# The pairwise adds of x squared, moved from VectorE to GpSimd in a fused two-layer kernel

## The chip, the cores and the metric
One core of one Trainium2 chip runs the kernel. The metric is device time in microseconds of one execution, the median of several runs. TensorE does the matrix products, VectorE and ScalarE the elementwise work, GpSimd (POOL in the rows) here only issues transfers, and SyncE (SP) issues most of the loads.

## What is computed
The input x has 512 tokens of 2048 features; it is kept as 16 tiles of 128 features by 512 tokens. Two layers follow each other. The first normalises x and mixes it with window means:

```python
h = rms_norm(x) * (1.0 + scale) + shift          # scale, shift, gate come from c @ w_mod
u, g = jnp.split(h @ w_in, 2, axis=-1)
pooled = windows' means of u minus u             # 4 groups, windows 2, 4, 8, 16
y = einsum(pooled, w_grp) * pool_scale
x = x + gate * ((y * silu(g)) @ w_out)
```

The second has three attentions, one of which reads 256 memory tokens:

```python
mkv = rms_norm_2(mem, mem_norm_gain) @ w_mem_kv
mk, mv = jnp.split(mkv, 2, axis=-1)              # 4 heads of 128; mk is normalised per head
```

What this case is about is the beginning: the eight panels of the product for mk and mv (the memory panels), and beside them the sum over the features of x * x, which `rms_norm(x)` of the first layer needs.

## The kernel before
Every weight is an fp32 panel that comes in four quarters of 128 by 512. A quarter is split into a rounded high part, made by ScalarE (`split_hi`, line 406), and a rest, made by VectorE (`split_lo`, line 416). TensorE then does three products for each 128 by 128 tile (`tile_products`, lines 422 to 424): high by high, high weight by low input, low weight by high input. The split runs three quarters ahead of its use: `split_hi` for quarter s waits until TensorE has used quarter s - 4, and `split_lo` waits for `split_hi`. Both engines work through their instructions strictly in the order in which the program lists them; semaphores join the engines.

At the start there are eight memory panels, n = 0 to 7; four give keys (one head each) and four give values. Each panel has four steps, s = 0 to 3, on each engine. I call the stretch of one panel on VectorE a beat. For n from 1 to 4 VectorE does in a beat:

- s = 0: `split_lo`; `mem_result` scales the product of the panel before (line 1659, `mem_plain`); from n = 2 `mem_keys` finishes the key norm (lines 473 and 475) and writes `mem_out` (line 1676).
- s = 1: `split_lo`, then `mod_column`, one product with a row sum over 2048 columns (lines 1614 and 1615), for the modulation of the first layer.
- s = 2: `split_lo`, then `mem_variance` (line 1608), whose drain is line 1669.
- s = 3: `split_lo`, then `add_square_of_x(2n - 1)` (line 1682).

ScalarE's beat has the four `split_hi`, the squares of a key panel (line 1251), two squares of x (`square_of_x(2n - 2)` and `(2n - 1)`, line 1265; each covers two tiles of x, 128 by 1024) and, at s = 3, `rstd_guess`, three instructions of lines 464, 466 and 468 that wait for the variance. In `x_squares` there are four places. The add number p = 1, 3, 5, 7 adds square p onto square p - 1.

TensorE sums each added pair over the features with a matrix of ones: `x_pair(j)` of line 1060 runs in panel n = j + 2 between its first and second quarter, and waits for `x_square_added` to reach j + 1. After the fourth, VectorE makes the variance of x in panel 5, ScalarE its root (`rstd_guess`), and in panel 6 VectorE scales the first tiles of x by it. TensorE cannot start the first layer's products (the `front` stage) without these.

GpSimd's queue at this time: the constants, the row of c, then a loop over the eight stores of keys and values, each of which waits for `mem_k_ready` or `mem_v_ready` and issues one transfer (line 2187).

Of the kernel before, what the change touches and what calls it, by code (L numbers as in the profile page):

```python
# [9 lines left out]
ALU = mybir.AluOpType  # L10
# [145 lines left out]
def program(nc, stream, wmod, cvec, xT, memT, cols_in, const_in, dist_in, x_store, c_store, mkv_store, sig_store, silu_store, out):  # L156
    ctx = ExitStack()
    with ctx:
        def sem(name):
            return ctx.enter_context(nc.semaphore(name))  # L160
# [11 lines left out]
        def sb(name, shape, dt, at):  # L172
            return nc.alloc_sbuf_tensor_at(name, shape, dt, offset=at)
# [98 lines left out]
        x_squares = sb("x_squares", [P, 4, 2 * T], F32, at_x1 + 32 * KB)  # L272
# [48 lines left out]
        x_square_ready, x_square_added = sem("x_square_ready"), sem("x_square_added")  # L321
# [86 lines left out]
        def split_lo(dve, t):  # L408

            s = t + 3  # L410
            dve.drain()  # L411
            if s.i is None and s.c >= TOTAL:
                return
            q = s.c % 4
            dve.wait_ge(hi_ready, (s + 1).value())
            nc.vector.tensor_tensor(w_lo[:, q, :], raw_quarter(s), w_hi[:, q, :].bitcast(F32),  # L416
                                    ALU.subtract).then_inc(lo_ready, 1)
# [52 lines left out]
        def rstd_newton(dve, dst, width, m):  # L470

            dve.wait_ge(rs_ready, (m + 1).value())
            nc.vector.scalar_tensor_tensor(rs_sq[:, :width], rs_sq[:, :width], -0.5, var[:, :width], ALU.mult, ALU.mult)
            dve.drain()
            nc.vector.scalar_tensor_tensor(dst, rs_sq[:, :width], 1.5, rs[:, :width], ALU.add, ALU.mult)
            dve.drain()
# [427 lines left out]
        def mem_kind(n):  # L904

            return None if n == 0 else "k" if n <= HEADS_C else "v"
# [690 lines left out]
        def _(dve):  # L1597
# [9 lines left out]
            def variance(source, width, features):  # L1607
                nc.vector.tensor_scalar(var[:, :width], source, 1.0 / features, EPS, ALU.mult, ALU.add).then_inc(var_ready, 1)
# [46 lines left out]
            def mem_result(n):  # L1655

                dve.wait_ge(w_used, 4 * n)
                dve.wait_ge(misc_full, max(n - 2, 0) + ONE)
                nc.vector.tensor_tensor(mem_plain[:, (n - 1) % 2, :], acc[(n - 1) % 2][:, :MEM], r_mem[:, :],
                                        ALU.mult).then_inc(mem_plain_ready, 1)  # L1660
                dve.drain().then_inc(acc_free[(n - 1) % 2], 1)
                if mem_kind(n) == "v":
                    dve.drain().then_inc(msrc_ready, 1)

            def mem_variance(n):

                dve.wait_ge(misc_full, n + ONE)
                variance(misc[:, :MEM], MEM, P)
                dve.drain().then_inc(misc_free, 1)

            def mem_keys(n):

                rstd_newton(dve, rs[:, :MEM], MEM, At(n))
                if n > 2:
                    dve.wait_ge(mem_out_stored[(n - 1) % 2], 16 * ((n - 1) // 2))
                nc.vector.scalar_tensor_tensor(mem_out[:, (n - 1) % 2, :], mem_plain[:, (n - 1) % 2, :], col("kg_c"),
                                               rs[:, :MEM], ALU.mult, ALU.mult).then_inc(mem_k_ready, 1)

            def add_square_of_x(p):

                dve.wait_ge(x_square_ready, p + 1)
                nc.vector.tensor_tensor(x_squares[:, p % 4 - 1, :], x_squares[:, p % 4 - 1, :], x_squares[:, p % 4, :],
                                        ALU.add).then_inc(x_square_added, 1)

            def scale_rows(k):

                nc.vector.tensor_tensor(x3[:, k, :], x3[:, k, :], r_x[:, :], ALU.mult).then_inc(xr_ready, 1)
# [7 lines left out]
            for n in range(2 * HEADS_C):  # L1695
                for s in range(4):
                    split_lo(dve, At(4 * n + s))
                    if n == 0 and s == 3:
                        dve.wait_ge(mem_sum_full, 4)
                        variance(score[0][:, :MEM], MEM, D)  # L1700
                    if n == 1 and s == 0:
                        rstd_newton(dve, r_mem[:, :], MEM, At(0))
                        dve.wait_ge(c_copied, 16)
                        dve.wait_ge(consts_loaded, 16 * 5)
                    if n > 0 and s == 0:
                        mem_result(n)
                    if 2 <= n <= 5 and s == 0:
                        mem_keys(n - 1)
                    if mem_kind(n) == "k" and s == 2:
                        mem_variance(n)  # L1710
                    if 1 <= n <= 4 and s == 3:
                        add_square_of_x(2 * n - 1)
                    if 1 <= n <= 4 and s == 1:
                        mod_column(n - 1)
                    if n == 4 and s == 1:
                        mod_biases(0, 4, 1.0).then_inc(scale_ready, 1)
                    if n == 5 and s == 2:
                        dve.wait_ge(x_pair_summed, 4)
                        variance(score[1][:, :], T, D)
                    if n == 6 and s == 0:  # L1720
                        rstd_newton(dve, r_x[:, :], T, At(5))
                        for k in range(4):
                            scale_rows(k)
                    if n == 6 and s == 3:
                        scaled_low(0)
                        scaled_low(1)
                    if n == 7 and s == 0:
                        scaled_low(2)
                        scaled_low(3)
# [126 lines left out]
            for i in range(2):  # L1856
                for s in range(4):
                    split_lo(dve, At(4 * (FIRST["group_b"] + i) + s))
                    n = 2 + 4 * i + s
# [308 lines left out]
        @block.gpsimd  # L2168
        def _(pool):

            for name, dst in (("ident", ident), ("blocks", blocks), ("slopes", slopes)):
                a, b = CONST[name]
                pool.dma_start(dst[:, :], const_in[:, a:b]).then_inc(consts_loaded, 16)
            a, b = CONST["edges"]
            pool.dma_start(edges[:, :, :].rearrange("p a b -> p (a b)"), const_in[:, a:b]).then_inc(consts_loaded, 16)
            a, b = CONST["causal"]
            pool.dma_start(causal[:, :], const_in[:, a:b]).then_inc(consts_loaded, 16)
            pool.wait_ge(c_ready, 1)
            pool.dma_start(silu_store, c_rows[:1, :]).then_inc(c_spread, 16)
            pool.wait_ge(c_spread, 16)  # L2180
            pool.dma_start(c_rows[:, :], silu_store.to_broadcast([P, D])).then_inc(c_copied, 16)
            for i in range(2 * HEADS_C):
                if i < HEADS_C:
                    pool.wait_ge(mem_k_ready, i + 1)
                else:
                    pool.wait_ge(mem_v_ready, i + 1 - HEADS_C)
                pool.dma_start(mkv_store[i, :, :], mem_out[:, i % 2, :]).then_inc(mem_out_stored[i % 2], 16)

            pool.wait_ge(yg_made, 8)
            for n in range(KT):  # L2190
                m = 2 * KT + n
                if n >= 2:
                    pool.wait_ge(wmod_used, m - 1)
                pool.dma_start(wmod_sb[MOD_SLOT[m]][:, :], wmod[m * P:(m + 1) * P, :]).then_inc(wmod_loaded[MOD_SLOT[m]], 16)

            for k in range(KT):
                pool.wait_ge(x1_ready, k + 1)
                pool.dma_start(x_store[k, :, :], x3[:, k, :]).then_inc(x1_stored[k // 2], 16)

            def sigmoid_store(m, n, b, slot):  # L2200

                pool.wait_ge(sig_made, (m + 1).value())
                pool.dma_start(sig_store[n.pick(), b, :, :].rearrange("a p t -> p (a t)"),
                               logits[slot][:, :]).then_inc(sig_stored[slot], 16)
            for b in range(3):
                sigmoid_store(At(b), At(1), b, b % 2)
            with steps(pool, 0, PAIRS // 3) as i:
                for b in range(3):
                    for e in range(2):
                        sigmoid_store(At(3 + 2 * b + e, 6, i), At(2 + e, 2, i), b, e)  # L2210
            pool.wait_ge(c_neg_ready, 1)
            pool.dma_start(c_store, f_a[:HEADS_B, :]).then_inc(c_stored, 16)
            pool.wait_ge(c_stored, 16)
            forget_rows(pool, At(0))
            windows(pool, pool_window)
# [106 lines left out]
```

## Time and profile before

| | us |
|---|---|
| three runs: lowest, median, highest | 2161.60, 2167.94, 2169.49 |
| the profiled execution, device time | 2160.38 |
| its span in the trace | 2158.8 |
| TensorE busy in the span | 2127.1 (99%) |
| VectorE busy | 1539.2 (71%) |
| ScalarE busy | 893.5 (41%) |
| GpSimd busy | 61.6 (3%) |
| one add of squares on VectorE, four in all | 1.22 each |

The span is what the trace covers; the profiled execution took 1.6 us more than it. Busy shares are means over stages that differ: the memory panels take the first 85 us, the rest of the span goes to the two layers. Times of TensorE's instructions are modelled at their ends, so its starts are the safer numbers.

### The profile page before, as it was taken

To read this page: it belongs to the slowest core of one execution; us is meant where nothing else is said; L and a number is where in the kernel's file an instruction comes from. 1 tells how busy PE (TensorE), PEld (TensorE's weight loads), DVE (VectorE), ACT (ScalarE), POOL (GpSimd) and SP (SyncE) were. 2 spreads that over 40 slices of the span, in tenths; PEclk is the share of its full clock that TensorE was granted. 3 is DMA by queue.
4 is the path that set the end of the run, shared out by engine and by line. 5 is a ranking of instruction groups with operands and counts; after the bars stand their busy time and mean duration, and the time that the engine had idled before them with its cause. 6 is when DMAs were issued, how large, how long until landed. Compare 5 with 4: busy or idle time off the path is not lost.

```text
span 2158.8 us, 34650 instructions
## 1 busy us (share of the span) xinstructions
PE 2127.1 (99%) x11664; PEld 1822.1 (84%) x11664; DVE 1539.2 (71%) x2580; ACT 893.5 (41%) x1573; POOL 61.6 (3%) x117
## 2 busy tenths in 40 slices
PE   7999999999999999999999999999999999999999
PEld 6788888888888999999997888888787887888887
DVE  7888877785658888888867666666777776665333
ACT  6433454433335444444443444444545444222221
POOL 0000000000000000000000000000000000000000
PEclk9999999999999999999999999999999999999999
DMA  9766423674444433433432222222222223554443
GB/s 381 276 228 247 169 92 98 230 269 141 145 146 132 147 133 113 144 133 114 142 105 95 91 87 88 92 88 83 69 88 69 89 88 120 168 169 152 143 145 111
DMA packets 83684, 303.26 MB, mean 140 GB/s; under 512 B 9317, under 2 KB 11765, under 8 KB 75265
## 3 DMA queue, kind: packets, MB, share of 16 engines
q1 hardware_dynamic: 71568, 258.24, 35.7%
q0 software_dynamic: 9280, 39.33, 5.3%
q10 hardware_dynamic: 2738, 4.47, 0.5%
q8 instruction: 51, 0.84, 0.2%
q14 instruction: 47, 0.39, 0.1%
HBM read 280.74 MB, written 21.27 MB: 140 GB/s over the span
## 4 chain that ended last, share of the span: by engine, by line
PE 80%; DVE 6%; ACT 4%; DMA 3%; issue 3%; DVEq 3%; ACTq 1%; POOL 0%; SPq 0%; POOLq 0%
PE bank L422 19%; PE bank L423 19%; PE bank L424 19%; PE bank L1163 6%; PE bank L1165 6%; PE bank L1164 6%; DMA w_raw<-stream 3%; DVE w_lo L416 3%; ACT w_hi L406 1%; PE bank L545 1%; PE bank L576 1%; DVEq L411 1%; PE bank L558 1%; ACT probs L626 1%; PE bank L1047 0%
## 5 line engine op out<-in xcount | busy, mean ns | idle before, releaser
L422 PE MATMUL bank<-x_hi,w_hi 128*128 128x512 f32 x2224 | 876.9, 394 | 5.2 <-DVEq L680 1.9
L424 PE MATMUL bank<-x_hi,w_lo 128*128 128x512 f32 x2224 | 866.7, 390 | 0.0
L423 PE MATMUL bank<-x_lo,w_hi 128*128 128x512 f32 x2224 | 866.4, 390 | 0.0
L416 DVE TENSOR_TENSOR w_lo<-w_raw,w_hi 128x512 fp32r<-128x512 f32 x524 | 362.9, 692 | 443.7 <-ACT w_hi L406 420.2
L406 ACT ACTIVATE w_hi<-w_raw 128x512 fp32r<-128x512 f32 x524 | 331.3, 632 | 690.1 <-PE bank L424 562.0
L422 PEld LDWEIGHTS bank<-x_hi,w_hi 128*128 128x128 f32 x2224 | 417.8, 188 | 103.2 <-issue 7.8
L424 PEld LDWEIGHTS bank<-x_hi,w_lo 128*128 128x128 f32 x2224 | 417.8, 188 | 88.1
L423 PEld LDWEIGHTS bank<-x_lo,w_hi 128*128 128x128 f32 x2224 | 418.2, 188 | 84.3 <-issue 0.2
L1163 PE MATMUL bank<-x_hi,pw_hi 128*128 128x256 f32 x1176 | 333.1, 283 | 0.9 <-DVE pw_lo L1936 0.8
L1164 PE MATMUL bank<-x_lo,pw_hi 128*128 128x256 f32 x1176 | 332.8, 283 | 0.0
L1165 PE MATMUL bank<-x_hi,pw_lo 128*128 128x256 f32 x1176 | 332.8, 283 | 0.0
L1163 PEld LDWEIGHTS bank<-x_hi,pw_hi 128*128 128x128 f32 x1176 | 225.8, 192 | 1.7 <-DVE pw_lo L1936 1.0
L1164 PEld LDWEIGHTS bank<-x_lo,pw_hi 128*128 128x128 f32 x1176 | 225.8, 192 | 0.0
L1165 PEld LDWEIGHTS bank<-x_hi,pw_lo 128*128 128x128 f32 x1176 | 225.8, 192 | 0.0
L1455 ACT ACTIVATE pw_hi<-w_sum 128x1024 fp32r<-128x1024 f32 x84 | 89.1, 1061 | 136.9 <-PE bank L1165 121.4
L1936 DVE TENSOR_TENSOR pw_lo<-w_sum,pw_hi 128x1024 fp32r<-128x1024 f32 x84 | 102.9, 1225 | 12.2 <-issue 10.1
L1615 DVE CUSTOM_DVE_ANT_0 wmod<-wmod,c_rows 128x2048 f32<-128x2048 f32 x48 | 109.8, 2286 | 0.0
L1455 ACT ACTIVATE pw_hi<-pw_raw 128x1024 fp32r<-128x1024 f32 x63 | 66.8, 1061 | 100.1 <-PE bank L1165 99.9
L1936 DVE TENSOR_TENSOR pw_lo<-pw_raw,pw_hi 128x1024 fp32r<-128x1024 f32 x63 | 77.2, 1225 | 9.5 <-issue 5.3
L626 ACT ACTIVATE probs<-probs,neg_max 128x256 f32<-128x256 f32 (+3 forms) x112 | 57.1, 510 | 45.4 <-DVE neg_max L701 45.4
L406 ACT ACTIVATE w_hi<-front_raw 128x512 fp32r<-128x512 f32 x64 | 40.5, 632 | 64.9 <-PE bank L424 57.6
L416 DVE TENSOR_TENSOR w_lo<-front_raw,w_hi 128x512 fp32r<-128x512 f32 x64 | 44.3, 692 | 23.1 <-ACT w_hi L406 18.8
(200 smaller groups left out, 1761.1 us busy)
## 6 DMA issues: line engine op xcount, KB each, us to landing
w_raw<-stream SPq DMA_DIRECT2D x262, 512.0 KB, 3.8
pw_raw<-stream SPq DMA_DIRECT2D x84, 512.0 KB, 4.6
wmod<-w_mod_rows SPq DMA_DIRECT2D x32, 1024.0 KB, 6.6
front_raw<-stream SPq DMA_DIRECT2D x16, 1024.0 KB, 9.8
wmod<-w_mod_rows POOLq DMA_DIRECT2D x16, 1024.0 KB, 5.7
sig_store<-logits POOLq DMA_DIRECT2D x45, 256.0 KB, 2.6
sig_back<-sig_store SPq DMA_DIRECT2D x8, 768.0 KB, 5.5
gate_sig<-sig_store SPq DMA_DIRECT2D x7, 768.0 KB, 5.9
```

Source lines behind the costliest of these rows:

```text
L406: nc.scalar.activation(w_hi[:, q, :], raw_quarter(s), ACT.Copy).then_inc(hi_ready, 1)
L416: nc.vector.tensor_tensor(w_lo[:, q, :], raw_quarter(s), w_hi[:, q, :].bitcast(F32), ALU.subtract).then_inc(lo_ready, 1)
L422: nc.tensor.matmul(bank_ap[:, :tokens], hi, x_hi[:, kx, :], start=start, stop=False)
L423: nc.tensor.matmul(bank_ap[:, :tokens], hi, x_lo[:, kx, :], start=False, stop=False)
L424: return nc.tensor.matmul(bank_ap[:, :tokens], lo, x_hi[:, kx, :], start=False, stop=stop)
L626: nc.scalar.activation(seg, seg, ACT.Exp, bias=neg_max[:, k:k + 1], scale=-1.0, accum_out=den[:, k:k + 1]).then_inc(exp_done, 1)
L1163: nc.tensor.matmul(to, hi, x_hi[:, 2 * k + odd, tokens], start=k == 0, stop=False)
L1164: nc.tensor.matmul(to, hi, x_lo[:, 2 * k + odd, tokens], start=False, stop=False)
L1165: mm = nc.tensor.matmul(to, lo, x_hi[:, 2 * k + odd, tokens], start=False, stop=k == 7)
L1455: nc.scalar.activation(pw_hi[f.slot][:, :], source[:, :], ACT.Copy).then_inc(pw_hi_ready, 1)
L1615: nc.vector.tensor_tensor_reduce(out=wmod_sb[slot][:, :], in0=wmod_sb[slot][:, :], in1=c_rows[:, :], scale=1.0, scalar=0.0, op0=ALU.mult, ...
L1936: nc.vector.tensor_tensor(pw_lo[f.slot][:, :], source[:, :], pw_hi[f.slot][:, :].bitcast(F32), ALU.subtract).then_inc(pw_lo_ready, 1)
```

## The change
The function `add_square_of_x` goes from VectorE's program to GpSimd's. The waits, the operands and the semaphore that it raises stay as they are. On VectorE its place at s = 3 of panels 1 to 4 falls away. On GpSimd the add number 2i + 1 stands in front of the wait for key i, in the loop of stores.

```diff
             def add_square_of_x(p):
 
-                dve.wait_ge(x_square_ready, p + 1)
-                nc.vector.tensor_tensor(x_squares[:, p % 4 - 1, :], x_squares[:, p % 4 - 1, :], x_squares[:, p % 4, :],
-                                        ALU.add).then_inc(x_square_added, 1)
...
-                    if 1 <= n <= 4 and s == 3:
-                        add_square_of_x(2 * n - 1)
...
+            def add_square_of_x(p):
+
+                pool.wait_ge(x_square_ready, p + 1)
+                nc.gpsimd.tensor_tensor(x_squares[:, p % 4 - 1, :], x_squares[:, p % 4 - 1, :], x_squares[:, p % 4, :],
+                                        ALU.add).then_inc(x_square_added, 1)
             for i in range(2 * HEADS_C):
                 if i < HEADS_C:
+                    add_square_of_x(2 * i + 1)
                     pool.wait_ge(mem_k_ready, i + 1)
```

## Rows read from the trace of the kernel before

**Rows 1.** The page: span, and each engine's busy us, share, instructions.
```profile
span 2158.8 us, 34650 instructions
PE 2127.1 (99%) x11664; PEld 1822.1 (84%) x11664; DVE 1539.2 (71%) x2580; ACT 893.5 (41%) x1573; POOL 61.6 (3%) x117
```
**Rows 2.** Stages: us; busy us (count) of PE, PEld, DVE, ACT, POOL; clock, DMA, GB/s.
```profile
64.00:86.00 22.00, 18.12 (x144) 17.36 (x143) 16.77 (x28) 12.34 (x21) 2.16 (x4) 1.00 0.91 353
86.00:176.00 90.00, 89.66 (x394) 73.25 (x393) 73.53 (x111) 29.14 (x47) 0.54 (x1) 1.00 0.59 214
```
**Rows 3.** Chain that ended last, one beat: start us, us, what.
```profile
40.84 0.69 DVE w_lo L416
...
41.90 0.42 ACT rs L464
...
43.42 0.64 ACT w_hi L406
...
49.84 0.69 DVE w_lo L416
```
**Rows 4.** VectorE in time: start us, us, engine, line, instruction [idle before <- releaser].
```profile
38.45 2.29 DVE L1615 CUSTOM_DVE_ANT_0 wmod<-wmod,c_rows 128x2048 f32<-128x2048 f32 x1
...
42.05 0.69 DVE L416 TENSOR_TENSOR w_lo<-front_raw,w_hi 128x512 fp32r<-128x512 f32 x1 [0.18 <-issue]
42.66 1.22 DVE L1682 TENSOR_TENSOR x_squares<-x_squares 128x1024 f32<-128x1024 f32 x1
44.08 0.69 DVE L416 TENSOR_TENSOR w_lo<-front_raw,w_hi 128x512 fp32r<-128x512 f32 x1 [0.21 <-ACT w_hi L406]
```
**Rows 5.** TensorE in time, same columns, ahead of the last pair sum.
```profile
60.68 0.28 PE L423 MATMUL bank<-memn_lo,w_hi 128*128 128x256 f32 x1
60.80 0.28 PE L424 MATMUL bank<-memn_hi,w_lo 128*128 128x256 f32 x1
62.19 1.98 PE L1060 MATMUL bank<-x_squares,ones 128*128 128x512 f32 x4 [1.11 <-DVE x_squares L1682]
```
**Rows 6.** Chain that ended last, from the last pair sum to the root.
```profile
62.19 1.98 PE bank L1060 x4
...
67.45 0.80 ACTq L1258
68.37 0.63 ACT rs L464
```
**Rows 7.** ScalarE in time: squares of x, and splits that wait for TensorE.
```profile
30.39 1.05 ACT L1265 ACTIVATE x_squares<-x 128x1024 f32<-128x1024 f32 x1
...
38.65 1.05 ACT L1265 ACTIVATE x_squares<-x 128x1024 f32<-128x1024 f32 x1
...
56.98 1.04 ACT L1265 ACTIVATE x_squares<-x 128x1024 f32<-128x1024 f32 x1
...
65.69 0.63 ACT L406 ACTIVATE w_hi<-front_raw 128x512 fp32r<-128x512 f32 x1 [2.62 <-PE bank L424]
67.35 0.63 ACT L406 ACTIVATE w_hi<-front_raw 128x512 fp32r<-128x512 f32 x1 [1.02 <-PE bank L424]
```
**Rows 8.** In time: a memset of one column on GpSimd, and one on VectorE.
```profile
0.49 0.10 POOL L2313 MEMSET const-float32-0.0<- 128x1 f32 x1 [0.49 <-issue]
...
38.48 0.06 DVE L1614 MEMSET arrived<- 128x1 f32 x1
```
**Rows 9.** Groups by line: instruction, count, then busy us, mean ns, idle before.
```profile
L823 DVE RECIPROCAL z_exp<-z_exp 128x256 f32<-128x256 f32 x16 | 28.0, 1752 | 2.0
```
**Rows 10.** GpSimd in time: the store of the first keys.
```profile
38.05 0.55 POOL L2187 DMA_DIRECT2D mkv_store<-mem_out  x1 [26.32 <-DVE mem_out L1676]
```
**Rows 11.** VectorE in time, panel 5: splits, and the variance of x.
```profile
65.19 0.69 DVE L416 TENSOR_TENSOR w_lo<-front_raw,w_hi 128x512 fp32r<-128x512 f32 x1
66.36 0.69 DVE L416 TENSOR_TENSOR w_lo<-front_raw,w_hi 128x512 fp32r<-128x512 f32 x1 [0.47 <-ACT w_hi L406]
66.97 0.68 DVE L1608 TENSOR_SCALAR var<-bank 128x512 f32<-128x512 f32 x1
```

More of the change, by code:

```diff
@@ L1677, in mem_keys @@
                                                rs[:, :MEM], ALU.mult, ALU.mult).then_inc(mem_k_ready, 1)
-            def add_square_of_x(p):
-                dve.wait_ge(x_square_ready, p + 1)
-                nc.vector.tensor_tensor(x_squares[:, p % 4 - 1, :], x_squares[:, p % 4 - 1, :], x_squares[:, p % 4, :],
-                                        ALU.add).then_inc(x_square_added, 1)
             def scale_rows(k):
```

## The prediction

> **What bounds the kernel now.** I read the page first: TensorE is busy 99% of the span, GpSimd 3% [rows 1]. So time can only come from the few places where TensorE stands still. The table by stages shows where: from 64 to 86 us, at the end of the memory panels, TensorE is busy 18.12 of 22.00 us, while from 86 to 176 us it is busy 89.66 of 90.00 [rows 2]. The edit lies wholly in the first part, so only the memory panels have time to give, and what they give or take should arrive undiminished at the end, since the later stages run at TensorE's own pace.
>
> Next the chain that ended last, for one beat. It goes from VectorE's third split at 40.84 us over the variance to ScalarE's root (41.90), its split (43.42), and back to VectorE, up to the next third split at 49.84 [rows 3]. The period is 49.84 - 40.84 = 9.00 us. The reader should see what is missing: the add of squares is not in this loop. VectorE does the add from 42.66 to 43.88, just while ScalarE works on the root; the split that follows starts at 44.08 because ScalarE's split ends at 43.42 + 0.64 = 44.06, and its row names ScalarE as the releaser [rows 3, 4].
>
> The add matters at another place. TensorE waits for it: the last ordinary product ahead of the fourth pair sum starts at 60.80, the pair sum itself at 62.19, released by the add [rows 5]. Products of this kind start 0.12 us apart [rows 5], so TensorE was ready at 60.92 and lost 1.27 us. It loses about as much in each of the four beats, but in the first three the loop of VectorE and ScalarE is the later one, so the loss is free. After the fourth, the chain runs through the pair sum to the root of x at 68.37 [rows 6].
>
> **The change part by part.** Removed: four adds of 1.22 us on VectorE [rows 4], 4.9 us of busy time. In the loop they are worth nothing: behind the removed add, the split waits for ScalarE until 44.06 as before. The cover is ScalarE's root, and it hides the whole add with 0.2 us to spare.
>
> Added: four adds on GpSimd. The trace has no elementwise work of this size there, so I bound one add from both sides. The lower end is VectorE's own 1.22 us. The upper end is the slowest elementwise work per column that the trace shows, a reciprocal of 256 columns in 1.752 us [rows 9]: 6.84 ns a column, or 7.0 us for 1024. Between them I go by the one kind of instruction that both engines ran: a memset of one column took 0.10 us on GpSimd and 0.06 on VectorE [rows 8]. 1.22 x 0.10 / 0.06 gives 2.0 us, an estimate, and I take that. The Trainium skill, GPSIMD Engine Reference, section 3.1, gives 4497 ns for an add of two fp32 inputs of 2048 columns on GpSimd; by it one add here would be an estimated 2.25 us, and the sum below would not move.
>
> When can it start? The last pair of squares is complete at 56.98 + 1.04 = 58.02 us [rows 7]. VectorE begins its add only at the end of its beat; GpSimd can begin at once, so it ends at 58.1 + 2.0 = 60.1, ahead of TensorE's 60.92. The wait of 1.27 us is gone whenever one add takes less than 60.92 - 58.1 = 2.8 us.
>
> The place in GpSimd's queue: each add stands ahead of the wait for a key. Behind the first add is the store of the first keys, issued at 38.05 [rows 10]; the first add is ready to start at 30.39 + 1.05 = 31.44 [rows 7] and ends at about 33.5, so the store is not delayed. The second add's squares are complete at 38.65 + 1.05 = 39.70 [rows 7], after that store has been issued (38.60). No transfer is added, and no queue of SyncE or ScalarE is touched.
>
> What is late next, with TensorE 1.27 us earlier? Two of ScalarE's splits in panel 5 waited for TensorE, at 65.69 and 67.35 [rows 7]. The second would start at 66.08, and the root, which stands behind it, at 68.37 - 1.27 = 67.10. VectorE's side must give the variance by then. Its split at 65.19 stays, since it follows the key norm; the next could start 0.61 us later (the spacing of 42.05 and 42.66 in [rows 4]), at 65.80 in place of 66.36, and the variance 0.61 after that, at 66.41, ending at 67.09 [rows 11]. So the root can start at about 67.15, and the gain is 68.37 - 67.15 = 1.2 us. VectorE is nearly the next to bind. From there on everything hangs on the root and moves with it.
>
> **The sum.** The profiled execution took 2160.38 us, its span 2158.8. Removed in the loop 0.0, added 0.0, at the exit -1.2: 2159.2 us. The profiled execution lies 7.6 us under the median of the three runs shown, 2167.94, which spread from 2161.60 to 2169.49. Against the median the forecast is 2167.9 - 1.2 = 2166.7 us.
>
> **The rivals.**
>
> Rival one, slower: VectorE and GpSimd can't read their operands side by side. Nothing in this trace shows the two at work on SBUF data together, so no row excludes it. Mechanism: the squares are complete at 39.70, in the middle of VectorE's product of 2048 columns, 38.45 to 40.74 [rows 4, 7]. GpSimd waits until 40.74, takes its turn for 2.0 us, and VectorE's third split, due at 40.84, starts only at about 42.75. That split is in the loop [rows 3], so the beat grows by 1.9 us. Panels 2, 3 and 4 have the same order of work, so it happens in each. Price 3 x 1.9 - 1.2 = +4.5 us, 2172.4. In panel 1 the squares end at 31.44 [rows 7], between two instructions of VectorE, and that could add 1.9 more: 2174.3. It decides as soon as GpSimd's turn comes ahead of the third split; if VectorE keeps the turn until its variance, which has only one operand in SBUF, the add falls into the time in which VectorE waits for ScalarE anyway, and 0.2 to 0.4 us a beat remain, so that the net is about nothing. The lock itself is what the Trainium skill states (SBUF — State Buffer, section Who interferes with whom): a VectorE instruction with two SBUF inputs and a GpSimd instruction that reads SBUF exclude each other for the whole instruction. No run here shows it yet.
>
> Rival two: the add is much slower than I take it. Then a second loop binds: pair sum to ScalarE's split 65.69 - 62.19 = 3.5 us [rows 5, 7], split and square 0.63 + 1.05 = 1.7, add T: a period of 5.2 + T. It exceeds 9.0 from T = 3.8. At the upper end, T = 7.0, the fourth pair sum starts at 31.5 + 7.0 + 3 x 12.2 = 75.1 in place of 62.2: +12.9 us, 2180.8. Against it: the bound comes from an iterative operation, far from an add. A first add alone that is late, by code that has to be fetched, costs nothing up to 2 us and then one for one.
>
> Rival three: the change does what it says on the engines, but the 1.2 us is lost again in the tail, where VectorE is nearly bound and splits of 64 to 86 us wait on one another. Then 2167.9.
>
> **How the numbers follow.** The forecast has 0.45, rival one 0.33, rival two 0.07, rival three 0.15. A change of 0.5% is 10.8 us, about what a measurement of this kernel can tell from no change. The forecast, rival one and rival three all lie within it (-1.2, +4.5 to +6.4, 0). Only rival two passes it, from T = 6.5 (31.5 + T + 3 x (5.2 + T) = 62.2 + 10.8), and the runs' own spread of 7.9 us can carry rival one over it, or the forecast under the lower edge: faster 0.02, same 0.91, slower 0.07. The range reaches from the forecast less most of that spread, 2161, to rival one's upper figure, 2175.
>
> **What would show it.** In the changed profile: VectorE's busy time down by 4.9 us; GpSimd's adds near 2.0 us each, starting at 31.5, 39.8, 48 to 49.5 and 58.1; TensorE's wait ahead of its four pair sums gone; third splits of VectorE still 9.0 us apart; the root of x at about 67.15. Third splits 11 us apart, with a hole behind the product of 2048 columns, would be rival one. Pair sums that wait for GpSimd would be rival two. A root at 67.15 with the first products of the front stage unmoved would be rival three. I am wrong on the sum if VectorE's instructions grow longer wherever GpSimd adds.

## The result, and the profile after

The changed kernel takes 2170.47 us (median of 20 runs, 2165.18 to 2177.81) against 2165.10 us (20 runs, 2158.90 to 2169.49) before: the ratio is 1.0028, 95% interval 1.0018 to 1.0037. It is slower by 0.28%, or 3.9 to 8.0 us. The forecast was 1.2 us faster; the time is that of rival one, which said +4.5 to +6.4.

The page of the changed kernel, the lines that answer to [rows 1]:

```profile
span 2165.8 us, 34652 instructions
PE 2126.5 (98%) x11664; PEld 1821.5 (84%) x11664; DVE 1543.3 (71%) x2576; ACT 893.7 (41%) x1573; POOL 75.1 (3%) x121
```

Four instructions of 1.22 us have left VectorE (2580 to 2576), and yet it is busy 4.1 us longer. So its other instructions have grown by 4.1 + 4.9 = 9.0 us. The splits of these panels (line 416) account for 5.6 us of that and the bias instruction of line 1624 for 2.0; of the rest, 1.0 us lies behind the memory panels, where the edit touches nothing. GpSimd is busy 13.5 us longer for four adds, 3.4 us each, where I had taken 2.0. Both at once is the sign that each stands in the other's way.

VectorE in time, from panels 1 to 4 of the changed kernel; it answers to [rows 3, 4]:

```profile
32.28 0.42 DVE L1608 TENSOR_SCALAR var<-bank 128x256 f32<-128x256 f32 x1
32.88 3.06 DVE L416 TENSOR_TENSOR w_lo<-front_raw,w_hi 128x512 fp32r<-128x512 f32 x2 [0.18 <-issue]
...
38.62 2.29 DVE L1615 CUSTOM_DVE_ANT_0 wmod<-wmod,c_rows 128x2048 f32<-128x2048 f32 x1
...
41.01 2.70 DVE L416 TENSOR_TENSOR w_lo<-front_raw,w_hi 128x512 fp32r<-128x512 f32 x1
...
46.27 0.69 DVE L416 TENSOR_TENSOR w_lo<-front_raw,w_hi 128x512 fp32r<-128x512 f32 x1 [1.35 <-ACT w_hi L406]
...
52.02 2.67 DVE L416 TENSOR_TENSOR w_lo<-front_raw,w_hi 128x512 fp32r<-128x512 f32 x1
...
63.01 2.14 DVE L1624 SCALAR_TENSOR_TENSOR mod<-mod_part,cols 128x4 f32<-128x4 f32 x1
65.24 0.69 DVE L416 TENSOR_TENSOR w_lo<-front_raw,w_hi 128x512 fp32r<-128x512 f32 x1
```

And GpSimd:

```profile
31.68 2.93 POOL L2178 TENSOR_TENSOR x_squares<-x_squares 128x1024 f32<-128x1024 f32 x1 [19.25 <-ACT x_squares L1265]
...
39.84 3.31 POOL L2178 TENSOR_TENSOR x_squares<-x_squares 128x1024 f32<-128x1024 f32 x1 [1.05 <-ACT x_squares L1265]
...
50.50 3.65 POOL L2178 TENSOR_TENSOR x_squares<-x_squares 128x1024 f32<-128x1024 f32 x1 [0.72 <-ACT x_squares L1265]
...
61.48 3.65 POOL L2178 TENSOR_TENSOR x_squares<-x_squares 128x1024 f32<-128x1024 f32 x1 [0.72 <-ACT x_squares L1265]
```

Read the two together. GpSimd's second add begins at 39.84, in VectorE's product of 2048 columns (38.62 to 40.91), and ends at 43.15. VectorE's third split starts at 41.01 and ends at 43.71, 2.70 us for work of 0.69. The product, which was first, keeps its length; the add waits for its end; then the split waits for the add. 43.15 - 40.91 = 2.24 us is the add's own time, as counted from the end of the product. The split's extra 2.01 us is in the loop: the next third split comes at 52.02, 11.01 us later in place of 9.00 [rows 3]. In panel 4 the instruction behind the product is one of 4 columns for the biases, and that takes 2.14 us in place of 0.16: the length of the victim does not matter.

The way out of the memory panels, on TensorE and ScalarE, answers to [rows 5, 6, 7]:

```profile
65.18 1.99 PE L1060 MATMUL bank<-x_squares,ones 128*128 128x512 f32 x4 [1.41 <-POOL x_squares L2178]
```

```profile
71.66 0.63 ACT L406 ACTIVATE w_hi<-front_raw 128x512 fp32r<-128x512 f32 x1 [1.68 <-PE bank L424]
72.20 0.36 ACT L1257 ACTIVATE mem_out<-bank 128x256 f32<-128x256 f32 x1
73.45 0.63 ACT L464 ACTIVATE rs<-var 128x512 f32<-128x512 f32 x1 [0.88 <-DVE var L1608]
```

The root of x starts at 73.45 (68.37 before), and VectorE's variance, no longer TensorE, is what it waits for. TensorE does wait for GpSimd's adds (1.41 us ahead of the fourth pair sum), but the chain that ended last does not run through that wait: it goes over VectorE's splits to the variance.

To compare heads of traces, I count from VectorE's first `mem_plain` (line 1659), which comes before anything that the change touches, to the first product of the front stage on TensorE. Before this is 85.00 - 27.90 = 57.10 us, after it is 90.22 - 28.06 = 62.16: the head is 5.06 us longer, inside the interval of the total. The rest, from the front stage to the end of the span, is 2158.8 - 85.0 = 2073.8 us before and 2075.6 after; over all the profiles below it lies between 2073.8 and 2081.9 and does not follow the edits. So the head is the measure for the small steps, and the totals only confirm the large one. Each head is read from one execution; the one kernel that was profiled twice gave heads 0.35 us apart (e9 and e10 below say why).

### The profile page after: what moved, and what is told of

The parts are those of the page before. It is cut to its first block, busy times and chain, and to the rows that moved or that the text cites. A ratio compares the mean times of both kernels' runs of the same rounds, so it can differ in the third digit from the quotient of the medians.

```text
span 2165.8 us, 34652 instructions
## 1 busy us (share of the span) xinstructions
PE 2126.5 (98%) x11664; PEld 1821.5 (84%) x11664; DVE 1543.3 (71%) x2576; ACT 893.7 (41%) x1573; POOL 75.1 (3%) x121
## 4 chain that ended last, share of the span: by engine, by line
PE 80%; DVE 8%; ACT 4%; DVEq 3%; DMA 2%; issue 2%; ACTq 1%; SPq 0%
PE bank L422 19%; PE bank L424 19%; PE bank L423 19%; PE bank L1163 6%; PE bank L1165 6%; PE bank L1164 6%; DVE w_lo L416 3%; DMA w_raw<-stream 1%; ACT w_hi L406 1%; PE bank L545 1%; PE bank L576 1%; DVEq L411 1%; PE bank L558 1%; DVE wsum L1753 1%; ACT probs L626 1%
## 5 line engine op out<-in xcount | busy, mean ns | idle before, releaser
L416 DVE TENSOR_TENSOR w_lo<-front_raw,w_hi 128x512 fp32r<-128x512 f32 x64 | 49.9, 779 | 24.9 <-ACT w_hi L406 20.2
```

## The experiments

Theory S says that VectorE and GpSimd take turns in reading SBUF, so that an instruction of the one waits for a whole instruction of the other. Against it stand: the order of waits in GpSimd's queue does it (Q), any work of GpSimd does it (W), only two operands on both sides collide (T), or an add on GpSimd is simply too slow here (L).

### Nothing added (e1_no_add)

```diff
-                nc.gpsimd.tensor_tensor(x_squares[:, p % 4 - 1, :], x_squares[:, p % 4 - 1, :], x_squares[:, p % 4, :],
-                                        ALU.add).then_inc(x_square_added, 1)
+                nc.gpsimd.memset(x_squares[:, p % 4, :1], 0.0).then_inc(x_square_added, 1)
```

> The changed kernel, but GpSimd's add is replaced by a memset of one column, so that the sums of x squared leave out half of the squares; the waits and the semaphore stay. Theory S (GpSimd and VectorE take turns in reading SBUF): with nothing read, VectorE's third splits stay at 0.69 us, beats are at 9.0 us, and the term of the forecast shows alone: the root of x at about 67.15 and the first product of the front stage at about 83.8 (before: 68.37 and 85.00; changed: 73.45 and 90.22), total 1.2 us under before. Theory Q (the loss comes from the new order of waits in GpSimd's queue, not from the add): the third splits or the pair sums are still late and the front stage starts near 90.

Measured: third splits of 0.69 us throughout, head 56.86 us (from 27.68 to 84.54), ratio to before 1.0003 (0.9988 to 1.0018). Theory Q falls: the same waits in the same queue cost nothing. But the head is only 0.24 us under before, not 1.2. From the third split of panel 4 (59.55) to the root of x (67.77) 1.06 us is gained, against 68.37 - 59.09 = 9.28 us before. Of that 0.67 us is lost again between the third splits of panels 2, 3 and 4, which start 9.10 and 9.82 us apart where they were 9.00 and 9.25, and 0.14 us between the root and the front stage. TensorE shows where the 0.67 comes from:

```profile
47.05 1.17 PE L585 MATMUL bank<-msrc,ones 128*128 128x256 f32 x2 [2.39 <-ACT msrc L1251]
47.65 0.78 PE L422 MATMUL bank<-memn_hi,w_hi 128*128 128x256 f32 x1
...
48.44 0.41 PE L424 MATMUL bank<-memn_hi,w_lo 128*128 128x256 f32 x1
48.65 0.41 PE L422 MATMUL bank<-memn_hi,w_hi 128*128 128x256 f32 x1
```

Stages of the same kernel: busy us (count) of each engine, then TensorE's granted clock, DMA share, GB/s:

```profile
44.00:48.00 4.00, 1.61 (x9) 1.24 (x7) 3.51 (x8) 1.88 (x3) 0.55 (x1) 0.89 1.02 420
48.00:52.00 4.00, 4.00 (x25) 3.99 (x24) 3.17 (x5) 2.68 (x5) 0.10 (x1) 0.68 1.02 424
52.00:56.00 4.00, 4.00 (x25) 3.04 (x24) 2.35 (x6) 3.30 (x6) 0.00 (x0) 1.00 0.71 254
```

TensorE, freed from the pair sum's wait, arrives early at the next wait and stands there for 2.39 us at one go, behind ScalarE, which had waited 2.22 us for a weight panel:

```profile
46.06 0.63 ACT L406 ACTIVATE w_hi<-front_raw 128x512 fp32r<-128x512 f32 x1 [2.22 <-DMA front_raw<-stream]
```

After that the granted clock is at its lower level (1.2 GHz of 2.4): products start 0.21 us apart in place of 0.12, for about 3 us. In the kernel before, TensorE stood still in smaller pieces, 0.77 us ahead of the first pair sum and 1.18 us ahead of the second (the latter at 43.93), did not wait at this place at all, and the clock stayed at 1.00 throughout. The load sets this pace: it released the same split at 45.73 before, so what TensorE had gained by then it could only spend on waiting. So, as I read it, the removed waits came back in one piece. At the lower clock TensorE then holds up ScalarE's split of panel 3 (50.83, after a wait of 1.17 us for TensorE) and with it the root of the panel.

### GpSimd writes and does not read (e2_write_only)

```diff
-                nc.gpsimd.tensor_tensor(x_squares[:, p % 4 - 1, :], x_squares[:, p % 4 - 1, :], x_squares[:, p % 4, :],
-                                        ALU.add).then_inc(x_square_added, 1)
+                nc.gpsimd.memset(x_squares[:, p % 4, :], 0.0).then_inc(x_square_added, 1)
```

> The changed kernel with a memset of 128 by 1024 on GpSimd in place of the add, onto the odd square of the pair, which is then left out of the sum. GpSimd writes as much and reads nothing. Theory S: no turn is taken, third splits 0.69 us, front stage at about 83.8. Theory W (any work of GpSimd on SBUF, writing too, shuts VectorE out): third splits grow by about the memset's length, perhaps 1 us, front stage near 87.

Measured: head 56.33 us (27.54 to 83.87), ratio 0.9996 (0.9980 to 1.0011). The memset lies in the middle of the product, on GpSimd and on VectorE:

```profile
38.94 0.96 POOL L2178 MEMSET x_squares<- 128x1024 f32 x1 [0.70 <-ACT x_squares L1265]
```

```profile
38.10 2.29 DVE L1615 CUSTOM_DVE_ANT_0 wmod<-wmod,c_rows 128x2048 f32<-128x2048 f32 x1
...
40.49 0.69 DVE L416 TENSOR_TENSOR w_lo<-front_raw,w_hi 128x512 fp32r<-128x512 f32 x1
```

It is done in 0.96 us, without waiting for the product's end, and the product keeps its 2.29. Theory W falls. The root of x came at 67.10 where the forecast had 67.15, but that is in part luck, as this trace started 0.36 us earlier than before (first `mem_plain` at 27.54 against 27.90). Counted from there the head gains 0.77 us: 0.92 us from the third split of panel 4 to the root, less 0.14 us between the root and the front stage. The third splits (40.49, 49.49, 58.74) stand 9.00 and 9.25 us apart, as before. This kernel's clock also dipped, to 0.61 from 48 to 52 us, but the beats do not show it; my estimate is that it cost at most the 0.14 us that the way to the root gained less than in e1, where the chain went over VectorE, while here it goes over TensorE.

### GpSimd reads one operand (e3_read_one)

```diff
-                nc.gpsimd.tensor_tensor(x_squares[:, p % 4 - 1, :], x_squares[:, p % 4 - 1, :], x_squares[:, p % 4, :],
-                                        ALU.add).then_inc(x_square_added, 1)
+                nc.gpsimd.tensor_copy(x_squares[:, p % 4, :], x_squares[:, p % 4 - 1, :]).then_inc(x_square_added, 1)
```

> The changed kernel with a copy of 128 by 1024 on GpSimd in place of the add, from the even square onto the odd one; the odd squares are left out of the sum. GpSimd reads one operand in place of two. Theory S: it waits for the end of the product of 2048 columns and then holds the third split up for its own length (some 1.1 us if one operand takes half as long as two), so that three beats grow by that and the front stage starts at about 83.8 + 3 x 1.0 = 87. Theory T (only two operands on both sides collide): third splits 0.69, front stage at 83.8.

Measured: head 58.14 us (27.58 to 85.72), ratio 1.0004 (0.9989 to 1.0019).

```profile
38.98 2.35 POOL L2178 COPY x_squares<-x_squares 128x1024 f32<-128x1024 f32 x1 [0.70 <-ACT x_squares L1265]
```

```profile
38.14 2.29 DVE L1615 CUSTOM_DVE_ANT_0 wmod<-wmod,c_rows 128x2048 f32<-128x2048 f32 x1
...
40.52 1.34 DVE L416 TENSOR_TENSOR w_lo<-front_raw,w_hi 128x512 fp32r<-128x512 f32 x1
```

The copy begins at the same point as the memset of the run before, but ends only at 41.33, 0.90 us after the product; and the third split takes 1.34 us. Theory T falls: one operand that GpSimd reads is enough. I had the copy at 1.1 us where it is 0.9, and so the head at 87 where it is 85.72. Against the write-only kernel the head is 1.81 us longer, near 3 x 0.65, the split's extra time.

### The same add, its turn after the third split (e4_hold)

```diff
                 pool.wait_ge(x_square_ready, p + 1)
+                pool.wait_ge(lo_ready, 4 * ((p + 1) // 2) + 6)
```

> The changed kernel with one more wait in front of GpSimd's add: for VectorE's third split of the panel. The add is the same; only the order of turns changes. Theory S: third splits stay at 0.69, the add runs at 41.6 to 43.8 while ScalarE makes the root; now the fourth split is held up, from 42.05 to 43.8, and the next first split starts at 44.5 in place of 44.08: 0.4 us a beat, 1.3 in all, front stage at about 86 (before 85.00, changed 90.22), total within 1.5 us of before. Theory L (an add on GpSimd is simply too slow beside this loop, whatever its order): front stage near 90.

Measured: head 58.93 us (27.70 to 86.63), ratio 1.0006 (0.9989 to 1.0023). GpSimd, and the chain that ended last:

```profile
41.79 2.36 POOL L2179 TENSOR_TENSOR x_squares<-x_squares 128x1024 f32<-128x1024 f32 x1 [3.06 <-DVE w_lo L416]
```

```profile
40.94 0.69 DVE w_lo L416
...
42.15 2.54 DVE w_lo L416
...
47.55 0.69 DVE w_lo L416
...
50.55 0.69 DVE w_lo L416
```

With no two-operand instruction of VectorE under way when it starts, the add takes 2.36 us. The third split has its 0.69 again; the fourth is held up, mostly beside ScalarE's root, and the beat is 50.55 - 40.94 = 9.61 us: 0.61 over before, where the changed kernel lost 2.01. The expectation had 0.4, with an add of 2.2 us. Theory L falls as to the size: 3.2 of the 5.1 us came from which instruction was held up, not from GpSimd's speed. But even in this order GpSimd's add is 1.8 us dearer than VectorE's, for it shuts VectorE out for longer than VectorE itself needs to add.

### One add on GpSimd (e5_one_panel)

```diff
+                if p == 5:
+                    dve.wait_ge(x_square_added, 2)
...
-                    if 1 <= n <= 4 and s == 3:
+                    if n in (1, 3, 4) and s == 3:
                         add_square_of_x(2 * n - 1)
...
+                if i == 1:
+                    pool.wait_ge(x_square_ready, 4)
+                    nc.gpsimd.tensor_tensor(x_squares[:, 2, :], x_squares[:, 2, :], x_squares[:, 3, :],
+                                            ALU.add).then_inc(x_square_added, 1)
```

> The kernel before with only the second add (p = 3) on GpSimd; the adds 1, 5 and 7 stay on VectorE. Theory S: one third split, that at about 41 us, is held up by some 2.0 us and its beat grows from 9.0 to 11.0; all other beats are as before, so from VectorE's first mem_plain to the first product of the front stage it takes 57.1 + 2.0 = 59.1 us (before 57.10, changed 62.16). Theory A (the loss is one for the whole stretch, by a shift of the loads or of ScalarE): much more or less than a third of the changed kernel's loss.

(The added wait of VectorE keeps the third add behind GpSimd's; it was met long before, as GpSimd's ended at 42.99 and the third began at 53.67.) Measured: the third split at 40.84 took 2.70 us, no other grew; head 59.40 us (27.89 to 87.29), ratio 1.0013 (0.9997 to 1.0028). One add costs 2.30 us, close to the 2.0 expected. The beat itself grew by 2.02 us. Of the other 0.3 us, 0.25 lie between the third split of panel 4 and the root of x, and the trace shows a likely cause: TensorE waited 2.32 us for the next pair sum, and its clock was 0.58 from 56 to 60 us.

### The changed kernel without the product in front of the last add (e6_after_mod_late)

```diff
-                    if 1 <= n <= 4 and s == 1:
+                    if 1 <= n <= 3 and s == 1:
                         mod_column(n - 1)
-                    if n == 4 and s == 1:
+                    if n == 5 and s == 3:
+                        mod_column(3)
                         mod_biases(0, 4, 1.0).then_inc(scale_ready, 1)
```

> The changed kernel with VectorE's fourth product of 2048 columns, and the biases behind it, moved from panel 4 to the end of panel 5, where VectorE waited 2.1 us for the root of x. Theory S: GpSimd's fourth add has no long product in front of it and takes about 2.3 us in place of 3.65, and what it then holds up is the fourth split, beside ScalarE's root. From the first mem_plain to the front stage: 62.16 less about 3.5 = 58.7 us, where the pair sum on TensorE binds. If the turn-taking had nothing to do with the product, the add would stay at 3.65 us.

Measured: head 58.90 us (27.91 to 86.81).

```profile
50.35 3.65 POOL L2179 TENSOR_TENSOR x_squares<-x_squares 128x1024 f32<-128x1024 f32 x1 [0.72 <-ACT x_squares L1265]
61.34 2.39 POOL L2179 TENSOR_TENSOR x_squares<-x_squares 128x1024 f32<-128x1024 f32 x1 [0.72 <-ACT x_squares L1265]
```

The third add still has the product in front of it and takes 3.65 us; the fourth has not and takes 2.39. So GpSimd's extra 1.3 us is the wait for the product's end. The ratio of the total is 1.0032 (1.0016 to 1.0048, 6 runs), although the head is 3.3 us shorter than the changed kernel's; why the total did not follow stays open. (The profiled execution, 2163.07 us, was the fastest of the six; the others took 2168.05 to 2172.24.)

### Two edits on VectorE alone (e7_before_swap, e8_before_mod_late, both in e9 and e10)

The traces say that TensorE's wait for the fourth pair sum is the first thing to be had. It can be had without GpSimd, in the kernel before: by the add in front of the fourth split, or by the late product of the edit above.

```diff
                 for s in range(4):
+                    if 1 <= n <= 4 and s == 3:
+                        add_square_of_x(2 * n - 1)
                     split_lo(dve, At(4 * n + s))
```

> The kernel before, adds on VectorE, with each add in front of the fourth split instead of behind it. Nothing of GpSimd. The fourth pair sum can start 0.6 us earlier (61.6 in place of 62.19), the fourth split falls into the rest of ScalarE's root. From the first mem_plain to the front stage 57.10 - 0.6 = 56.5 us. If the loads of the weights bind more than the pair sum, no gain.

> The kernel before, adds on VectorE, with the fourth product of 2048 columns and the biases moved to the end of panel 5. VectorE's beat of panel 4 is 2.4 us shorter, TensorE's wait for the fourth pair sum (1.1 us) goes, and the product lies beside ScalarE's root of x. From the first mem_plain to the front stage 57.10 - 1.2 = 55.9 us; the total 1 us under before, below what these rounds can tell. If the loads bind, less.

Measured: heads 56.47 us (28.23 to 84.70) and 55.85 us (27.74 to 83.59), both as expected, to 0.1 us. The totals, 0.9990 (0.9977 to 1.0003) and 0.9998 (0.9984 to 1.0012), cannot tell 0.6 or 1.2 us from nothing. Then both together:

> The kernel before with both edits that helped the head alone: each add of squares on VectorE in front of the fourth split, and the fourth product of 2048 columns with its biases at the end of panel 5. Both remove the same wait of TensorE ahead of the fourth pair sum (1.1 us), so they don't add up: from VectorE's first mem_plain to the front stage 55.8 us (before 57.10, with the late product alone 55.85). The total about 1.2 us under before, too little to tell from it with these rounds. If the two gains are separate, 55.2.

Measured: head 55.55 us (27.72 to 83.27), ratio 0.9975 (0.9964 to 0.9987), more than the head has to give. I ran the same kernel once more:

> The same kernel as in the run before (adds in front of the fourth split, late fourth product), once more: there its ratio to before was 0.9975, 2.8 to 7.8 us, while the head of its trace is only 1.35 us shorter. If all of its gain lies in the head, the ratio comes back at 0.9994. If there is a gain behind the head too, 0.9975 comes again.

The 1.35 us in this text is a slip: 57.10 - 55.55 is 1.55 us, and a gain in the head alone would give 0.9993. Measured: head 55.20 us (27.71 to 82.91), ratio 0.9990 (0.9975 to 1.0005). The two intervals overlap between 0.9975 and 0.9987.

The 0.35 us between the two heads of one kernel was lost ahead of everything that the edits touch. Panel 1 begins so in e9, on TensorE and on VectorE:

```profile
29.00 0.70 PE L585 MATMUL bank<-msrc,ones 128*128 128x256 f32 x2 [2.01 <-ACT msrc L1251]
```

```profile
28.67 0.69 DVE L416 TENSOR_TENSOR w_lo<-front_raw,w_hi 128x512 fp32r<-128x512 f32 x1 [0.53 <-ACT w_hi L406]
```

and so in e10:

```profile
28.64 0.70 PE L585 MATMUL bank<-msrc,ones 128*128 128x256 f32 x2 [1.17 <-ACT msrc L1251]
```

```profile
28.32 0.69 DVE L416 TENSOR_TENSOR w_lo<-front_raw,w_hi 128x512 fp32r<-128x512 f32 x1 [0.18 <-issue]
```

In e9 a load was late: ScalarE's split in front of these, at 28.01, had waited 2.10 us for it, in e10 0.49 us. After the wait of 2.01 us TensorE's clock was 0.54 from 30 to 32 us and 0.60 from 32 to 34. From this split on the two traces keep that distance, to 0.01 us.

So 55.20 us is the head without that accident, and it is the figure that the expectation of e9 gave for two separate gains: 0.63 + 1.25 = 1.88 us, measured 1.90. The expectation that they do not add up was wrong. Once panel 4 is shorter (e8), TensorE's wait for the third pair sum, 0.86 us, reaches the loop: ScalarE's split at 56.28 waits 0.94 us for TensorE, and VectorE's third split at 56.95 waits 0.58 us for that. With the adds moved forward as well (e10) the wait for the third pair sum is 0.37 us, and the root of panel 4 starts 30.31 us after the first `mem_plain` in place of 30.94.

A gain of 1.55 and 1.90 us in the head stands in the two traces; whether there is more behind it is open. In the total the two edits together are shown to be faster than the kernel before in one set of runs and not in the other, both times by less than 0.4%; both sets lie under the changed kernel's ratio of 1.0028 (1.0018 to 1.0037).

## Why the prediction was wrong

**What bounds.** Right. The head is the only part that moved with the edits, the loop of 9.00 us is VectorE's and ScalarE's, and the add of squares is not in it: with the adds gone from VectorE and nothing on GpSimd that reads (e2) the third splits of panels 2 and 3 start at 40.49 and 49.49, 9.00 us apart.

**Removed, in the loop 0.0.** Right. The split behind it now waits 1.35 us for ScalarE, where it waited 0.21 [rows 4].

**Added, 0.0 in the loop.** This is the step that failed. I costed GpSimd's add by its length and asked only whether it ends before TensorE needs it. I took the two engines to be independent, because no row showed them together, and gave this 0.45 against 0.33 for the rival, though the one source that spoke of it, the Trainium skill, spoke against. Absence from the trace was no evidence either way; that rule should have had the larger chance. The traces agree with it wherever they test it (SBUF — State Buffer, section Who interferes with whom): with reads on both sides the later one waits for the whole of the earlier (e3, after), with writes only nobody waits (e2).

**The length of the add.** 2.0 us against 2.35 to 2.39 where it runs undisturbed (e4, e6) and 2.22 to 2.25 as counted from the end of the instruction that it waited for, a little short. It would not have changed the sum of the forecast, but sets the price of the turn.

**The exit, -1.2.** Right in size. In the changed kernel the time from the first split of panel 5 (68.49) to the root of x (73.45) is 4.96 us, before it is 68.37 - 62.34 = 6.03: 1.07 us gained, and VectorE's variance is next to bind, as said. In e8 the head is 1.25 us shorter. It is paid away here by the three turns. Two smaller things were put at nothing. The way from the root to the front stage was to stay as it was; it grew by 0.14 us in the changed kernel, e1 and e2. And the waits of TensorE in the first three beats were called free and about as long as the last; they were 0.77, 1.18 and 0.85 us against 1.11, and where they went, TensorE waited in one piece behind a load and its clock fell (e1, e2). So even without the turns the head gained 0.24 and 0.77 us there, not 1.2.

**Rival one.** Right in mechanism and place: the squares end within the product, GpSimd goes ahead of the third split. Its price was 3 x 1.9 - 1.2 = +4.5; measured in the head, 2.01 + 1.98 + 1.98 - 1.07 = +4.90 up to the root of x (4.92 as read there), and 0.14 more on the way to the front stage, 5.06 in all. The price that it held possible for panel 1 did not fall due: there VectorE's third split was first at 31.67, GpSimd at 31.68 waited for it (2.93 us), and what was held up was the fourth split, beside the root. The starts are 0.01 us apart. VectorE also had the first turn there in e6 (31.53 against 31.54) and in e3, where the copy's recorded start is even 0.01 us ahead of the split's; that it could have gone the other way is not shown.

**Rivals two and three.** Neither came. The changed kernel's pair sums did wait for GpSimd, 0.40 to 1.41 us, which was named as the sign of rival two, but none of these waits bound at an add of 2.3 us; in e4, with a wait of 1.71 us, the fourth did. Of the exit's gain of 1.07 us 0.14 was lost in the tail of the changed kernel.

## What to carry to other kernels

Before work is moved to an idle engine, ask what it shares with the busy one, and which instruction is next in line when it starts: the moved add cost nothing by its length and 2 us a beat by standing in front of a split that the loop waits for. If the two must share, let the moved work start where the victim has slack (e4 lost 1.8 us where the changed kernel lost 5.1), or reorder on the busy engine alone (e8 gained 1.25). When a wait is removed, look whether the pieces of idle time around it merge, for a longer wait can cost clock (e1). And check whether two gains that seem to remove one wait really do: together the two edits on VectorE gave the sum of what each gave alone, as a second wait had come to count.

## What the runs showed of the hardware

A GpSimd add of 128 by 1024 with two fp32 operands in SBUF takes 2.35 to 2.39 us undisturbed and 2.22 to 2.25 counted from the end of the instruction that it waited for, a copy counted so 0.90, a memset 0.96; VectorE's add takes 1.22. While GpSimd reads, a VectorE instruction with two operands in SBUF waits until it ends, whether it has 512 columns (0.69 to 2.70 us) or 4 (0.16 to 2.14); the profile counts this wait as busy time of the waiting instruction, on both engines, and names no releaser for it. The variance of panel 1, whose operand is in PSUM, kept its 0.42 us (32.28 to 32.70) beside GpSimd's add, which had its turn from the end of the third split, 32.36; in e4 that of panel 2 kept it too (41.55 to 41.97) with GpSimd's add begun at 41.79. I had not expected the clock: the one wait of 2.39 us of TensorE in e1 was followed by some 3 us at the lower level, while the four waits of 0.77 to 1.18 us ahead of the pair sums in the kernel before were not, nor was one of 1.70 us at 77.42. In e2, e3, e5 and e9 a single wait of 1.86 to 2.32 us likewise stood ahead of a stretch at the lower level. Whenever GpSimd waited for the product of 2048 columns, it had the next turn, although VectorE's following instruction came within 0.1 us of the product's end (panels 2 to 4 of the changed kernel).
